# Reading eight fp32 recurrent states in two batches of four column groups in a two-layer retention and RG-LRU step

## What is computed

```python
def step(S, inp):
    qc, kc, vc = inp
    scores = jnp.einsum('bhid,bhjd->bhij', qc, kc) * decay[None]
    inner = jnp.einsum('bhij,bhje->bhie', scores, vc)
    cross = jnp.einsum('bhid,bhde->bhie', qc, S) * q_dec[None, :, :, None]
    S_new = S * chunk_dec[None, :, None, None] + jnp.einsum(
        'bhjd,bhje->bhde', kc * k_dec[None, :, :, None], vc)
    return S_new, inner + cross
```

## Time and profile before

| | |
|---|---|
| median of 3 runs | 2565.28 us (2565.11 to 2570.04) |
| the profiled execution, its own time | 2560.41 us |
| its span in the profile | 2558.6 us |
| TensorE matmul busy | 2478.6 us, 97% |
| GpSimd busy | 1553.4 us, 61% |
| VectorE busy | 1342.7 us, 52% |
| ScalarE busy | 720.9 us, 28% |

### The profile page before, as it was taken

How to read it: one execution, slowest core, us unless ns; L and a number is a source line. 1 busy time by engine, 2 the same in 40 slices (tenths; PEclk the granted TensorE clock), 3 DMA queues, 4 the chain that set the end, 5 groups by cost and what they waited for, 6 DMA issues and landing times.

```text
span 2558.6 us, 52418 instructions
## 1 busy us (share of the span) xinstructions
PE 2478.6 (97%) x19636; PEld 2392.2 (93%) x19636; DVE 1342.7 (52%) x1715; ACT 720.9 (28%) x1109; POOL 1553.4 (61%) x1265
## 2 busy tenths in 40 slices
PE   7999999999999999999999999999999999999997
PEld 7898989999999999999998898989999999999997
DVE  8765656568744632022367565656786446221223
ACT  3414141437721111011124141414467112100111
POOL 5354645467676666666654545454777766666664
PEclk9999999999999999999999999999999999999998
DMA  5545454522233222232346363635222332222322
GB/s 193 198 142 197 148 201 135 197 84 88 81 99 92 93 91 83 91 98 83 91 156 231 112 235 108 235 108 198 82 83 87 97 96 92 91 81 94 94 84 85
DMA packets 121748, 315.69 MB, mean 123 GB/s; under 512 B 12192, under 2 KB 12960, under 8 KB 121568
## 3 DMA queue, kind: packets, MB, share of 16 engines
q1 hardware_dynamic: 60480, 199.78, 24.7%
q10 hardware_dynamic: 61088, 113.34, 13.0%
HBM read 272.69 MB, written 40.38 MB: 122 GB/s over the span
## 4 chain that ended last, share of the span: by engine, by line
PE 71%; DVE 9%; DVEq 6%; issue 4%; ACT 3%; DMA 2%; ACTq 2%; POOL 1%; POOLq 1%
PE proj L359 42%; PE aux L359 23%; PE aux L529 2%; DVE scratch L1086 2%; DVEq L1231 1%; PE aux L601 1%; POOL w_low L346 1%; PE aux L552 1%; DMA scratch<-in_sret 1%; DMA scratch<-v_rows 1%; PE aux L593 1%; DVE split_scratch L896 1%; POOLq L344 1%; DVE scratch L1144 1%; ACTq L1578 1%
## 5 line engine op out<-in xcount | busy, mean ns | idle before, releaser
L346 POOL TENSOR_TENSOR w_low<-w_raw,w_high 128x512 fp32r<-128x512 f32 (+2 forms) x840 | 1110.3, 1343 | 62.9 <-issue 3.1
L343 POOL TENSOR_SCALAR w_high<-w_raw 128x1024 fp32r<-128x1024 f32 (+3 forms) x420 | 442.7, 1054 | 918.4 <-PE proj L359 695.3
L359 PE MATMUL proj<-x_high,w_high 128*128 128x260 f32 x2752 | 560.6, 285 | 32.8 <-DVE x_low L743 13.6
L359 PE MATMUL proj<-x_high,w_low 128*128 128x260 f32 x2752 | 555.4, 283 | 0.0
L359 PE MATMUL proj<-x_low,w_high 128*128 128x260 f32 x2752 | 554.9, 283 | 0.0
L359 PEld LDWEIGHTS proj<-x_high,w_high 128*128 128x128 f32 x2752 | 428.1, 189 | 45.2 <-DVE x_low L743 14.0
L359 PE MATMUL proj<-split_scratch,w_high 128*128 128x260 f32 x2544 | 414.8, 285 | 17.4 <-DVE scratch L873 13.0
L359 PEld LDWEIGHTS proj<-x_high,w_low 128*128 128x128 f32 x2752 | 425.3, 189 | 0.0
L359 PEld LDWEIGHTS proj<-x_low,w_high 128*128 128x128 f32 x2752 | 424.9, 189 | 0.0
L359 PEld LDWEIGHTS proj<-split_scratch,w_high 128*128 128x128 f32 x2544 | 352.0, 190 | 25.2 <-DVE scratch L873 14.2
L359 PE MATMUL aux<-x_high,w_high 128*128 128x260 f32 x1344 | 272.0, 283 | 2.6 <-DVE residual L1223 1.4
(11 more groups left out here) (186 smaller groups left out, 2559.9 us busy)
## 6 DMA issues: line engine op xcount, KB each, us to landing
w_raw<-in_wstream SPq DMA_DIRECT2D x252, 512.0 KB, 3.5
scratch<-in_sret ACTq DMA_DIRECT2D x96, 512.0 KB, 6.5
out_ret_s<-scratch ACTq DMA_DIRECT2D x64, 512.0 KB, 3.8
w_raw<-in_wstream SPq DMA_DIRECT2D x72, 448.0 KB, 3.2
w_raw<-in_wstream SPq DMA_DIRECT2D x48, 384.0 KB, 3.0
scratch<-v_rows ACTq DMA_DIRECT2D x64, 256.0 KB, 5.2
w_raw<-in_wstream SPq DMA_DIRECT2D x48, 320.0 KB, 2.8
out_ret_p<-scratch ACTq DMA_DIRECT2D x8, 512.0 KB, 2.8
```

What stands on the lines that cost most here:

```text
L343: pool.tensor_scalar(WH[:, j, w], WR[:, j, w], 1.0, 0.0, ALU.mult, ALU.add)
L346: m = pool.tensor_tensor(WL[:, j, part], WR[:, j, part], WH[:, j, part].bitcast(F32), ALU.subtract)
L359: m = pe.matmul(out, wt[:, w, blk * P:(blk + 1) * P], x[xi], start=first and n == 0, stop=last and n == 2)
```

## The change

The state is no longer split. It moves through TensorE in fp32. The stationary operand `QZ` holds for each key half and each sample 32 columns of fp32 query, all zero but one. A batch is four samples, one in each buffer of the ring; sample r of a batch writes PSUM rows 32r to 32r+31, that is the r-th group of 32 columns of the array. Batch n puts sample 4n+r in row 32r+n. There are two batches of eight matmuls for a head. All 128 rows are copied out, and the selection matrix picks row 32r+n.

The scratch for the split state, ScalarE's high parts and VectorE's low parts go. The waits of a batch (`read_begin`: query columns ready, bank free, four loads landed) stand ahead of it: in the first head in the middle of value tiles 0 and 3, with the batches behind those tiles; in the others behind `ret_out` tile 1 and in the middle of value tile 1, with the batches behind `ret_out` tile 2 and value tile 1. ScalarE's queue issues the second four loads together when the first batch is done. A small scratch of the convolution state now shares an output buffer, and some copies and a memset ahead of the first layer differ.

```diff
-        SSH, SSL = rview(o, KT, DV), rview(o + KT * DV, KT, DV)
...
-        QP = sb("q_pairs", [P, KT, NS, 2 * NS], F32R)
+        QZ = sb("q_columns", [P, KT, NS, QUAD])
...
-                    def read_out(b):
-
-                        if b == 0:
+                    def read_begin(n):
+
+                        if n == 0:
                             if first:
                                 pe.wait_ge(s["t_free"], tb + (QK - 1))
-                            pe.wait_ge(s["qp_full"], hh + 1)
+                            pe.wait_ge(s["qz_full"], hh + 1)
                             aux_begin(hh, "RO")
+                        for r in range(SRING):
+                            pe.wait_ge(s_ld[r], hh * (16 * LOADS) + 16 * (n + 1))
+
+                    def read_out(n):
+
                         for d in range(KT):
-                            pe.wait_ge(s["s_low"], hh * (NS * KT) + (b * KT + d + 1))
-                            for n, part in enumerate((SSH, SSL)):
-                                m = pe.matmul(aux("RO", 2 * NS), QP[:, d, b, :], part[:, d, :],
-                                              start=b == d == n == 0, stop=b == NS - 1 and d == KT - 1 and n == 1)
-                            m.then_inc(s["ro_done"], 1)
+                            for r in range(SRING):
+                                m = pe.matmul(AUX[QUAD * r:QUAD * (r + 1), BANK["RO"], :],
+                                              QZ[:, d, SRING * n + r, :], SS[r][:, d, :],
+                                              start=n == d == 0, stop=n == NBAT - 1 and d == KT - 1)
+                        m.then_inc(s["ro_done"], 1)
...
-                        ret_out(hh, ub, QK, tb, QK, lambda m_: read_out(m_ // 2) if m_ % 2 else None)
+                        ret_out(hh, ub, QK, tb, QK,
+                                lambda m_: read_begin(0) if m_ == 1 else read_out(0) if m_ == 2 else None)
                         for i in range(VT):
-                            whole(ub, uv + i, tb, v0 + i, XH, XL)
-                            read_out(MT // 2 + i)
+                            whole(ub, uv + i, tb, v0 + i, XH, XL,
+                                  midway=lambda: read_begin(1) if i == 1 else None)
+                            if i == 1:
+                                read_out(1)
...
-                        state_low(0)
                         turn_odd(KT + 1)
                         turned(KF, lambda: ret_add(tb, QK, 0))
...
-                        if 1 <= b <= SRING:
-                            act.wait_ge(s["s_low"], (hh * NS + b) * KT)
-                            load_state(b - 1 + SRING)
+                    act.wait_ge(s["ro_done"], hh * NBAT + 1)
+                    for b in range(SRING, NS):
+                        load_state(b)
```

More of the change, by code:

```diff
@@ L115 @@
 LOADS = SUSES[0] + 1
+NBAT, QUAD = NS // SRING, P // SRING
+assert NBAT == 2
 UPDATED = [(u + SRING) % NS for u in range(NS)]
@@ L535, in one_head @@
                             whole(ub, uv + i, tb, v0 + i, XH, XL,
[L536 removed]
+                                  midway=lambda: read_begin(i // 3) if i in (0, 3) else None,
                                   freed_by=tb + (i + 1) if i < 2 else None)
[L538 to L540 removed]
+                            if i in (0, 3):
+                                read_out(i // 3)
+                    else:
+                        ret_out(hh, ub, QK, tb, QK,
+                                lambda m_: read_begin(0) if m_ == 1 else read_out(0) if m_ == 2 else None)
                         for i in range(VT):
[L542 to L543 removed]
+                            whole(ub, uv + i, tb, v0 + i, XH, XL,
+                                  midway=lambda: read_begin(1) if i == 1 else None)
+                            if i == 1:
+                                read_out(1)
                     pe.wait_ge(s["qk_low"], hh * 2 + 2)
                     for j in range(TT):
[L547 to L548 removed]
                         aux_begin(hh, f"SC{j}")
@@ L606, in samples @@
                     def samples():
-                        pe.matmul(aux("SEL", NS), PAIRG[0:2 * NS, :], ROS, start=True, stop=False)
+                        pe.matmul(aux("SEL", NS), PICKG[:], ROS, start=True, stop=False)
                         pe.matmul(aux("SEL", NS), DIAG[0:NS, :], VS, start=False, stop=True).then_inc(s["aux_mm"], 1)
@@ L751, in _ @@
             dve.wait_ge(s["setup_ld"], 16 * 4)
-            tt(PAIR[0:2 * NS, :], ID[0:2 * NS, 0:2 * NS:2], ID[0:2 * NS, 1:2 * NS:2], ALU.add)
+            for n in range(NBAT):
+                dve.tensor_copy(PICK[:, SRING * n:SRING * (n + 1)],
+                                ID[:, n:n + QUAD * (SRING - 1) + 1:QUAD])
+            dve.memset(QZ[:], 0.0)
             dve.tensor_copy(GAIN[:], NRM[:, 0, :])
@@ L886, in q_parts @@
                         dve.drain()
[L887 to L897, removed]
+                        for n in range(NBAT):
+                            m = dve.tensor_copy(QZ[:, :, SRING * n:SRING * (n + 1), n],
+                                                QF[:, :, SEQ + SRING * n:SEQ + SRING * (n + 1)])
+                        m.then_inc(s["qz_full"], 1)
                     def key_low():
@@ L917, in one_head @@
                         q_parts()
-                        state_low(0)
                         turned(KF, lambda: None)
                         dve.tensor_copy(GNC[:], CUR[:, bass.ds(head * VT + PC_GN, VT)])
-                        state_low(1)
-                        value(0)
                         key_low()
-                        for e in range(1, VT):
-                            state_low(2 * e)
+                        for e in range(VT):
                             value(e)
-                            state_low(2 * e + 1)
                     else:
@@ L1347, in load_vb @@
                                       ).then_inc(v_ld[u % VRING], 16)
[L1349 to L1355, removed]
                     act.dma_start(DEC[:], dec[bass.ds(head, 1)].rearrange("a p n -> (a p) n")
@@ L1365, in one_head @@
                     A(QH, QF, copy).then_inc(s["qk_high"], 1)
[L1366 to L1374, removed]
-                        if 1 <= b <= SRING:
-                            act.wait_ge(s["s_low"], (hh * NS + b) * KT)
-                            load_state(b - 1 + SRING)
+                    act.wait_ge(s["rope_done"], hh * 2 + 2)
+                    A(KH, KF, copy, scale=DK ** -0.5).then_inc(s["qk_high"], 1)
+                    if first:
+                        A(e_, CUR[:, PC_SP:PC_SP + LT], ACT.Abs)
+                        act.drain()
+                        A(e_, e_, ACT.Exp, scale=-1.0).then_inc(s["lam_exp"], 1)
+                    act.wait_ge(s["ro_done"], hh * NBAT + 1)
+                    for b in range(SRING, NS):
+                        load_state(b)
                     for i in range(TT // 2):
```

27 lines of the change are left out of this document (10 added, 17 removed).

## The result

The changed kernel takes 2519.36 us, median of 4 runs (2516.28 to 2522.43), against 2565.2 of the kernel before: ratio 0.9827, 95% interval 0.9816 to 0.9839, 45.8 us faster. A second series gave 2520.45 and 0.9829. The direction was forecast, the size was not: 13.8 us were forecast, and the time lies 2.3 us from the 2517.1 of the rival with four groups truly side by side. The profiled execution took 2516.28 us, its span is 2514.3.

A forecast was written before the change was run, and what follows sets the result against it. TensorE, busy 97% of the span, was taken as the bound. Terms +3.9 - 13.8 - 4.2 - 1.2 + 1.0 + 0.5 = -13.8 us gave 2546.6 from the profiled 2560.41, a median of 2551.5 us; range 2510 to 2571.

The forecast's parts named there:

- the rival with four groups truly side by side: Read-out batches overlap fourfold, 1.81 us each: -30.5 us in place of +3.9, 2517.1 us; chance 0.27.
- A read-out before: Old state read-out on TensorE: 0.93 us each, 64 of them, 59.5 us in all.
- a record of 0.43 us: One of the two matmul records each 512-column fp32 product leaves on TensorE, the second 0.43 us behind the first.
- the upper bound: Read-out batch with nothing overlapping: 6.97 us, +52.0 us for the read-out, 2599.6 us in all; chance 0.13.
- the change of kind: TensorE going from fp32 products back to fp32r work: 0.09 us added to each batch.
- The value taken between the bounds: Read-out batch with matmuls strictly in order, each product overlapping the next by one record: 3.96 us, +3.9 us in all.
- The wait that goes: TensorE's wait for VectorE's read of the second key tile, behind `ret_out` tile 0, vanishes: six times 2.3 us, -13.8 us.
- the clock: Lower granted clock behind that TensorE wait, in three of six heads, goes too: 3 x 1.4, -4.2 us.
- GpSimd's split as the next to be late: Weights for `ret_out` tile 2, split by GpSimd, would hold narrowly with 0.7 us of slack.
- the second four loads: State loads issued together behind batch 0, landing some 10 us later against 23 us available: no wait expected.
- Small terms: First-head low-part wait gone -1.2 us, new first-head wait for query columns +1.0, extra work at the start +0.5.
- the likeliest case: The forecast itself, with the in-order batch: 2543 to 2558 us; chance 0.46.

The follow-up runs named there:

- one group: Changed kernel with all eight samples of the read-out in column group 0, 32 rows copied out instead of 128: 2602.72 us, ratio 1.0156.
- swap: Changed kernel with each batch issued group by group, both key halves of one sample in a row: 2522.67 us, ratio 0.9841.
- deep_by_group: Changed kernel with each product cut into four of 128 columns, eight products of a group in a row: 2593.77 us, ratio 1.0126.
- the two on it: Two unused VectorE subtractions added to the changed kernel, 2539.57 us; state 0's low part moved behind the second key tile in the kernel before, 2548.32 us.
- the run with the wait put back: Changed kernel with two unused 128x512 subtractions on VectorE ahead of the second key tile: 2539.57 us, ratio 0.9902.
- the two small moves: Changed kernel with query columns copied ahead of the query's low part and TensorE's first-head wait right ahead of the batch: 2514.8 us, ratio 0.981.
- one line moved: Kernel before, with the low part of state 0 on VectorE moved behind the second key tile: 2548.32 us, ratio 0.9939.

## Why the prediction was wrong, point by point

- **A read-out before at 0.93 us, 59.5 us in all, and a record of 0.43 us:** right. From the first record to the next product one group took 6.98 us for the 6.97 of the upper bound, four groups 1.85 for the 1.81 of the lower. What the sum left out are the edges: 0.09 for the change of kind was taken from the end of the products in the earlier trace rows alone, though there too the first stands 0.33 us behind the pair ahead of it (103.94 to 104.27), not 0.24. With all edges a batch costs 2.05 us, 3.8 us more in 16 batches than the rival's 1.81.
- **The value taken between the bounds, the step that failed:** "If the engine takes matmuls strictly in order, group 1's first record can't start before group 0's second." It does start before. I read from the earlier trace rows that matmuls keep the program's order, but those records all go to the same columns, so the row could not tell an engine that keeps order for everything from one that keeps it for each column group. The term came out at -26.7 instead of +3.9, and that is nearly the whole miss of 32 us. The swapped order and the cut products show what stands in its place: a group holds one product behind the one that runs, and only a second one waiting blocks the others. The changed kernel never has more than that, since it takes the groups in turn.
- The statement of the Trainium skill that spoke for my value ("TensorE: Matmul & The Clock Gate", "The mechanism": strict order of starts and ends) holds in these traces only for the starts within one column group. The other ("TensorEngine Tiling (Array Packing)", "Theoretical Speedup": up to four times) is met in full in the steps of a batch, 16 to 4, and is 3.8 times from the first record to the next product, 6.98 to 1.85 us. The drain that its "Key Properties" announces can be no more than what a batch costs beyond its four steps, 2.05 - 4 x 0.43 = 0.33 us. Part of that is no drain for tiling, as the fp32 products of the earlier trace rows have 0.09 us of it on either side.
- **The wait that goes, -13.8, and the clock, -4.2:** right in place and cause, and in size within what the runs can tell: the two on it gave 16 and 19 us for 18.0 forecast. That three waits had the clock behind them was the draw of one execution: it was five in the run with the wait put back.
- **GpSimd's split as the next to be late:** it was not in head 1, as TensorE has no idle time in the stretch from 147.70 to 175.90 above, and over the run TensorE's waits for the split went from 10.4 to 11.0 us only. Nor did the second four loads, issued together, hold anything up: in head 1 they landed like this (ns for the issue, first and last start; then us to landing).

```profile
L1334 ACTq DMA_DIRECT2D scratch<-in_sret x4: 379/382/417, 155.8 to 157.4; - x4
...
DMA to landing us min/median/max: 3.9/7.0/8.9
```

- **Small terms:** the new wait in the first heads cost 1.5 us each, 3.0 in all, where I had taken 1.0 between 0 and 2. The copies were no quicker for being half as wide, and ended at 45.5, with GpSimd's instruction (see the two small moves), and the matmuls around a pause lose a little beyond it. The start cost 0.24, not 0.5, but TensorE's first wait varies by more than that between runs that share the start (11.7 and 12.2 us in the two traces of the kernel before and of it with one line moved).
- **The range and the chances:** the time lies in the full range of 2510 to 2571, near its low end, and outside the likeliest case's own 2543 to 2558. The case that came, four groups side by side, had a chance of 0.27. The evidence against it was one row on a single column group, which deserved less weight.

## What to carry to other kernels

fp32 products with at most 32 stationary columns are worth spreading over the column groups: with four groups in turn they cost about a quarter of what they cost in one (1.85 and 6.98 us for a batch), and a state that needs no split saves two engines their work. Issue the groups in turn, or with no more than two products of one group in a row. Before crediting such a rewrite, look at what the removed work delayed: here 16 to 19 of 46 us came from two instructions that stood ahead of a read that freed a PSUM slot, and one moved line gives that alone.

## What was not expected of the hardware

- The order of TensorE's matmuls is kept for each column group, not for the engine: a product whose columns are busy is held aside, one per group, and later products of other groups start 0.06 us or less behind (swap). The second one that waits blocks everything until the one held aside has started (in deep_by_group, 12 of 16 records alone, 1.32 us).
- Two tiny copies on VectorE took 1.1 to 1.4 us in 14 of the 16 heads of two runs and 0.24 in the other two. In the slow cases one of them lasted until GpSimd's running instruction ended (1.06 us, to 45.47, with GpSimd's end at 45.43). That is read from the timelines and not tested.
- Batches of 7 us with only 32 of 128 columns in use left the granted clock at its upper level, 2.4 GHz, while a pause of 2.2 us was followed by a stretch at the lower one in some heads and not in others: three of six in the kernel before, five of six with the wait put back.
